# VectorE's order in an attention stage: the combine of the older unit ahead of the row maximum of the newest

## The chip, the cores and the metric

One NeuronCore of a Trainium2 chip runs the whole program. The metric is the device time of one execution in microseconds (us).

## The reference, cut to what matters

The program computes two model blocks in a row on 512 tokens of width 1024 in fp32: an RWKV-7 layer with its feed-forward net, a differential attention layer with its feed-forward net, and then two layers of gated linear attention, spatial gating, retention and pooling. The change concerns the differential attention alone:

```python
s = einsum('bqhd,bkhd->bhqk', q_blk, k) * scale      # 16 half heads of 64
s = where(k_chunk <= q_chunk, s, -inf)               # chunks of 64 tokens
p = softmax(s, axis=-1).reshape(B, 8, 2, Q_BLOCK, S)
p = p[:, :, 0] - lam * p[:, :, 1]                    # the two halves of a head
o = einsum('bhqk,bkhe->bqhe', p, v)                  # v is 128 wide for a head
```

## The kernel before, in words

The kernel is written engine by engine; each engine has its own instruction list, and semaphores order them. The attention stage has 32 units (`N_UNITS`): 8 heads times 4 blocks of 128 queries. Unit i is head i // 4 and query block tq = i % 4 (`unit`, line 914); since the mask is causal in chunks it has tq + 1 key blocks of 128, so 128, 256, 384 or 512 keys. Both halves of the head are worked in one unit.

A unit passes through these steps:

- TensorE, `scores` (line 2836): the scores of both halves, into two PSUM banks (banks 4 and 5 for even units, 2 and 3 for odd ones, `unit_banks`, line 307). It waits until the exponentials of unit i - 2 have read those banks.
- VectorE, `row_max` (line 2142): waits for the scores, writes -1e30 over the masked corner (L2149), reduces both halves to their negative maximum (L2150) and scales it (L2151, `sc_max`).
- ScalarE: waits for `sc_max`, then one exponential for each half (L1586) with its sum as accumulator output; results go to `Pb` (six buffers: three units).
- VectorE, `combine` (line 2155): waits for the exponentials, takes the reciprocal of the second half's sum (L2161), multiplies by -lam and the first half's sum (L2162), and adds the scaled second half to the first (L2165, `pc_ready`). All is kept scaled by the first half's sum, which a later norm takes out.
- TensorE, `transposes` (line 2863): waits for `pc_ready`, transposes the combined block into PSUM bank 6 (L2867).
- ScalarE: copies the transposes to `PTs` (L1598).
- TensorE, `values` (line 2847): multiplies them with the values (L2856). After a head's fourth unit ScalarE copies the output (L1213) and squares it (L1602).

The order on each engine is written out by hand, one iteration p for each unit:

- TensorE (lines 2880 to 2901): half of a piece of the value projection (only p < 24), values(p - 2), the other half, scores(p + 1), transposes(p - 1); from p = 27 on a head sum (L2875) for a later norm.
- VectorE (lines 2168 to 2175): row_max(p), for p = 0 also two key scalings (`key_scale`), then combine(p - 1).
- ScalarE (lines 1570 to 1602): at p = 8, 16 and 24 a copy of projected values and at p = 0, 8 and 16 the rounding of a weight tile (L1202), then the exponentials of p, the output copy, the transposes' copy of p - 1, the squares.
- POOL computes the low part of each weight tile (L1081) once ScalarE has rounded it. SP only loads weights.

Woven into the first 24 units is the rest of the value projection (`value_part`, line 2813): 12 matmuls a unit.

Of the kernel before, what the change touches and what calls it, by code (L numbers as in the profile page):

```python
# [569 lines left out]
def build(nc, t, out):  # L570
# [3 lines left out]
    with ctx:  # L574
# [272 lines left out]
        def wait_job(eng, key):  # L847

            _, who, _, n = JB.info[key]
            eng.wait_ge(job_a if who == "A" else job_d, n)  # L850
# [63 lines left out]
        def unit(i):  # L914

            return i // UNITS_OF_HEAD, i % UNITS_OF_HEAD
# [812 lines left out]
        def _(dve):  # L1729
            seq = [0]  # L1730

            def link(ins):

                seq[0] += 1
                ins.then_inc(dve_seq, 1)
                dve.wait_ge(dve_seq, seq[0])
# [371 lines left out]
            def key_scale(k):  # L2108

                wait_done(dve, ("hinv", k))  # L2110
                dve.tensor_tensor(ak[:, k, :], ak[:, k, :], bank(job_banks(("hinv", k))[0]), ALU.mult
                                  ).then_inc(job_d, 1)
# [29 lines left out]
            def row_max(i):  # L2142

                hd, tq = unit(i)
                b = job_banks(("sc", i))[0]
                N = P * (tq + 1)
                q = 4 + 2 * (i % 3)
                wait_done(dve, ("sc", i))
                link(dve.memset(psum[0:64, b:b + 2, N - CH:N], -1e30))  # L2149
                link(dve.tensor_reduce(col[:, 14:16], psum[:, b:b + 2, 0:N], AX.X, ALU.max, negate=True))  # L2150
                dve.tensor_tensor(col[:, q:q + 2], col[:, 14:16], invq[:, tq, 2 * hd:2 * hd + 2], ALU.mult  # L2151
                                  ).then_inc(sc_max, 1)
                dve.wait_ge(sc_max, i + 1)

            def combine(i):

                hd, tq = unit(i)
                N = P * (tq + 1)
                q = 2 * (i % 3)
                wait_job(dve, ("sc", i))  # L2160
                link(dve.reciprocal(col[:, 17 + q:18 + q], col[:, 17 + q:18 + q]))  # L2161
                link(dve.scalar_tensor_tensor(out=col[:, 17 + q:18 + q], in0=col[:, 17 + q:18 + q],  # L2162
                                              scalar=col[:, 3:4], in1=l1s[:, tq, hd:hd + 1], op0=ALU.mult,
                                              op1=ALU.mult))
                dve.scalar_tensor_tensor(out=Pb[:, q, 0:N], in0=Pb[:, q + 1, 0:N], scalar=col[:, 17 + q:18 + q],  # L2165
                                         in1=Pb[:, q, 0:N], op0=ALU.mult, op1=ALU.add).then_inc(pc_ready, 1)

            for p in range(N_UNITS + 1):
                if p < N_UNITS:
                    row_max(p)  # L2170
                if p == 0:
                    key_scale(6)
                    key_scale(7)
                if p:
                    combine(p - 1)
            sums = l1s[:, :, :].rearrange("p t k -> p (t k)")[:, :, None]
            dve.scalar_tensor_tensor(out=lsq[:, :, :].rearrange("p t (k a) -> p (t k) a", a=2),
                                     in0=sums.to_broadcast([P, TT * HEADS // 2, 2]), scalar=1e-5 * P,
# [958 lines left out]
```

## Time and profile before

| | |
|---|---|
| median of 3 runs | 2244.77 us (2243.22 to 2253.79) |
| profiled execution | 2259.35 us, of it 2257.5 us span |
| busy share: TensorE, VectorE, ScalarE, POOL | 90%, 35%, 36%, 34% |
| attention stage | about 1151 to 1262 us of the span |
| mean granted TensorE clock, share of full | 0.946 |

Times inside a profile count from the start of the span. The busy share of an engine is an average over stages with different limits. PE is TensorE's matmul side, PEld its weight loads, DVE is VectorE, ACT is ScalarE.

### The profile page before, as it was taken

Reading aid. Unit: us, or ns where it says so; the run is one execution under the profiler, and the core shown is the slowest. Engines: PE = TensorE matmul, PEld = TensorE weight load, DVE = VectorE, ACT = ScalarE, POOL = GpSimd, SP = SyncE. Lnnn points to the kernel's source line nnn. Section 1 sums busy time; section 2 is a strip of 40 time slices with the busy share of each in tenths; the row PEclk is TensorE's granted clock in tenths of the full one; section 3 lists DMA queues with packets and bytes.
Section 4 is the critical chain, followed back from the end, with each engine's and each line's share of the span. In section 5 each row is a group of like instructions: output and inputs, shape, how many; then the busy total and the mean of one; then the engine's idle time right before and its main releaser. Section 6 shows DMA issues by size and latency. Waiting matters only on the chain.

```text
span 2257.5 us, 36581 instructions
## 1 busy us (share of the span) xinstructions
PE 2030.8 (90%) x15556; PEld 1559.9 (69%) x15556; DVE 794.1 (35%) x1186; ACT 816.4 (36%) x1056; POOL 774.9 (34%) x644
## 2 busy tenths in 40 slices
PE   5997976668999999989999899999998999969897
PEld 3666766544778888866577578888887876748664
DVE  5576433324322221025666442222002123252233
ACT  6765132232243432132256434343123222242232
POOL 3353322210334444334421134444444432234430
PEclk8998999985999999999999899999999998989999
DMA  4111000020223332312111023333223311122110
GB/s 152 56 50 61 2 4 4 4 61 9 75 75 93 93 101 94 102 58 82 58 55 38 19 75 93 95 92 106 89 84 94 94 46 48 38 79 77 55 56 37
DMA packets 190706, 147.09 MB, mean 65 GB/s; under 512 B 6888, under 2 KB 188351, under 8 KB 190576
## 3 DMA queue, kind: packets, MB, share of 16 engines
q1 hardware_dynamic: 190576, 145.18, 21.0%
q8 instruction: 104, 1.70, 0.3%
q14 instruction: 26, 0.21, 0.0%
HBM read 143.06 MB, written 2.10 MB: 64 GB/s over the span
## 4 chain that ended last, share of the span: by engine, by line
PE 79%; DVE 7%; ACT 5%; issue 4%; POOL 3%; DMA 1%; SPq 0%; ACTq 0%; DVEq 0%
PE psum L2402 21%; PE psum L2404 19%; PE psum L2403 19%; PE psum L2557 4%; POOL w_lo L1081 2%; DVE X_lo L1744 2%; ACT w_hi L1202 1%; PE psum L2478 1%; PE psum L2408 1%; PE psum L2843 1%; PE psum L2782 1%; PE psum L2856 1%; PE psum L2773 1%; PE psum L3044 1%; PE psum L3027 1%
## 5 line engine op out<-in xcount | busy, mean ns | idle before, releaser
L1081 POOL TENSOR_TENSOR w_lo<-weight_raw,w_hi 128x256 fp32r<-128x256 f32 (+5 forms) x588 | 703.4, 1227 | 1254.8 <-ACT w_hi L1202 1254.7
L2402 PE MATMUL psum<-X_hi,w_hi 128*128 128x512 f32 x1528 | 634.5, 415 | 52.6 <-DVE X_lo L1744 33.4
L2404 PE MATMUL psum<-X_hi,w_lo 128*128 128x512 f32 x1528 | 607.5, 398 | 0.0
L2403 PE MATMUL psum<-X_lo,w_hi 128*128 128x512 f32 x1528 | 607.0, 397 | 0.0
L2402 PEld LDWEIGHTS psum<-X_hi,w_hi 128*128 128x128 f32 x1528 | 294.4, 193 | 162.4 <-issue 85.7
L1202 ACT ACTIVATE w_hi<-weight_raw 128x2048 fp32r<-128x2048 f32 (+2 forms) x134 | 249.4, 1862 | 347.4 <-PE psum L2404 336.6
L2403 PEld LDWEIGHTS psum<-X_lo,w_hi 128*128 128x128 f32 x1528 | 294.8, 193 | 66.0 <-issue 8.5
L2404 PEld LDWEIGHTS psum<-X_hi,w_lo 128*128 128x128 f32 x1528 | 293.6, 192 | 64.4
L1793 DVE TENSOR_TENSOR sgate<-rt,psum 128x512 f32<-128x512 f32 x44 | 30.2, 687 | 320.5 <-PE psum L2404 320.5
L2402 PE MATMUL psum<-hb_hi,w_hi 128*128 128x512 f32 x352 | 136.9, 389 | 0.0
L2403 PE MATMUL psum<-hb_lo,w_hi 128*128 128x512 f32 x352 | 136.9, 389 | 0.0
L2404 PE MATMUL psum<-hb_hi,w_lo 128*128 128x512 f32 x352 | 136.9, 389 | 0.0
L2402 PE MATMUL psum<-w_hi,X_hi 128*128 128x256 f32 x384 | 116.3, 303 | 5.6 <-POOL w_lo L1081 3.6
L1187 ACT ACTIVATE sgate<-sgate 128x512 f32<-128x512 f32 x44 | 27.9, 635 | 255.2 <-DVE sgate L1793 255.2
L2403 PE MATMUL psum<-w_lo,X_hi 128*128 128x256 f32 x384 | 110.2, 287 | 0.0
L2404 PE MATMUL psum<-w_hi,X_lo 128*128 128x256 f32 x384 | 110.1, 287 | 0.0
L1783 DVE TENSOR_TENSOR x<-x,psum 128x512 f32<-128x512 f32 x32 | 20.5, 683 | 224.5 <-PE psum L2404 224.5
L2402 PEld LDWEIGHTS psum<-w_hi,X_hi 128*128 128x128 f32 x384 | 75.4, 196 | 12.8 <-issue 12.6
L2403 PEld LDWEIGHTS psum<-w_lo,X_hi 128*128 128x128 f32 x384 | 75.3, 196 | 0.6 <-issue 0.5
L2403 PEld LDWEIGHTS psum<-hb_lo,w_hi 128*128 128x128 f32 x352 | 66.1, 188 | 13.8
L2404 PEld LDWEIGHTS psum<-hb_hi,w_lo 128*128 128x128 f32 x352 | 66.1, 188 | 13.7
L2402 PEld LDWEIGHTS psum<-hb_hi,w_hi 128*128 128x128 f32 x352 | 66.1, 188 | 13.7
(454 smaller groups left out, 2599.7 us busy)
## 6 DMA issues: line engine op xcount, KB each, us to landing
weight_raw<-in_ffn_w_gu SPq DMA_DIRECT2D x88, 512.0 KB, 4.9
weight_raw<-in_l_w_in SPq DMA_DIRECT2D x45, 512.0 KB, 4.7
weight_raw<-in_ffn_w_down SPq DMA_DIRECT2D x40, 512.0 KB, 3.6
weight_raw<-in_kv_w SPq DMA_DIRECT2D x16, 512.0 KB, 4.4
weight_raw<-in_l_w_out SPq DMA_DIRECT2D x16, 512.0 KB, 4.3
weight_raw<-in_rw_w_k SPq DMA_DIRECT2D x8, 512.0 KB, 6.9
weight_raw<-in_rw_w_r SPq DMA_DIRECT2D x8, 512.0 KB, 4.1
weight_raw<-in_rw_w_v SPq DMA_DIRECT2D x8, 512.0 KB, 4.0
```

Of the source, the lines that this page charges most:

```text
L1081: ins = pool.tensor_tensor(l, r, h.bitcast(F32), ALU.subtract)
L1187: act.activation(sgate[:, j, :], sgate[:, j, :], ACT.Silu).then_inc(ff_gate, 1)
L1202: last = act.activation(h, r, ACT.Copy)
L1744: dve.tensor_tensor(X_lo[:, k, :], f, X_hi[:, k, :].bitcast(F32), ALU.subtract).then_inc(xlo_ready, 1)
L1793: dve.tensor_tensor(sgate[:, j, :], rt[:, :], bank(b[0]), ALU.mult).then_inc(ff_raw, 1)
L2402: pe.matmul(ps, wh, xh, start=start, stop=False, skip_group_check=True)
L2403: pe.matmul(ps, wh, xl, start=False, stop=False, skip_group_check=True)
L2404: return pe.matmul(ps, wl, xh, start=False, stop=stop, skip_group_check=True)
L2408: pe.matmul(ps, w, xx[0], start=True, stop=False, skip_group_check=True)
L2478: ins = pe.matmul(bank(6), c_("ones"), square_buffer(i)[:, k % 2, :], start=k == 0, stop=k == KT - 1)
L2557: ins = pe.matmul(out(q, r, k), left(q, r, k), right(q, r, k), start=True, stop=True, skip_group_check=True)
L2773: ins = pe.matmul(psum[0:16, job_banks(key)[0], :], c_("sel64", 16, 16 * i), oT[:, i, :], start=i == first, stop=i == last)
```

## The change

VectorE's loop over the units calls `combine(p - 1)` ahead of `row_max(p)`. The key scalings of p = 0 stay behind row_max(0). The other engines' lists, the semaphores and the buffers are the same.

```diff
             for p in range(N_UNITS + 1):
+                if p:
+                    combine(p - 1)
                 if p < N_UNITS:
                     row_max(p)
                 if p == 0:
                     key_scale(6)
                     key_scale(7)
-                if p:
-                    combine(p - 1)
```

## Rows read from the trace of the kernel before

**Rows 1.** The page's busy time, share of the span and instructions.
```profile
PE 2030.8 (90%) x15556; PEld 1559.9 (69%) x15556; DVE 794.1 (35%) x1186; ACT 816.4 (36%) x1056; POOL 774.9 (34%) x644
```

**Rows 2.** Busy time by stretch: length; engines' busy us (instructions); clock, DMA share, GB/s.
```profile
1215.90:1229.10 13.20, 13.00 (x95) 10.39 (x95) 8.34 (x24) 8.71 (x24) 0.00 (x0) 1.00 0.22 77
1229.10:1240.30 11.20, 9.11 (x58) 6.08 (x58) 8.31 (x24) 8.20 (x23) 0.00 (x0) 1.00 0.00 0
1240.30:1254.00 13.70, 12.44 (x54) 5.94 (x54) 8.37 (x25) 8.39 (x24) 0.00 (x0) 0.88 0.00 1
```

**Rows 3.** Waits, 1157 to 1262 us: us in total, times, longest.
```profile
DVE psum L2149 <- PE psum L2843: 26.4, 21, 2.7
...
PEld psum L2867 <- DVE Pb L2165: 11.7, 17, 1.1
...
PEld psum L2856 <- ACT PTs L1598: 8.1, 13, 0.9
```

**Rows 4.** VectorE's timeline around unit 15: start, us, instruction, idle before it.
```profile
1202.32 0.17 DVE L2149 MEMSET psum<- 64x128 f32 x1 [0.64 <-PE psum L2843]
...
1203.78 0.16 DVE L2151 TENSOR_TENSOR col<-col,invq 128x2 f32<-128x2 f32 x1
...
1205.92 0.16 DVE L2161 RECIPROCAL col<-col 128x1 f32<-128x1 f32 x1
...
1208.61 0.17 DVE L2149 MEMSET psum<- 64x128 f32 x1 [1.49 <-PE psum L2843]
```

**Rows 5.** ScalarE's timeline there: exponentials of unit 15, first of unit 16.
```profile
1203.97 0.78 ACT L1586 ACTIVATE Pb<-psum,col,invq 128x512 f32<-128x512 f32 x1 [0.97 <-DVE col L2151]
...
1205.40 0.20 ACT L1586 ACTIVATION_READ_ACCUMULATOR Pb<-psum,col,invq 128x1 f32 x1
...
1208.58 0.47 ACT L1586 ACTIVATE Pb<-psum,col,invq 128x128 f32<-128x128 f32 x1
```

**Rows 6.** Groups of instructions by shape in the stage: busy us, mean ns, idle before.
```profile
L2150 DVE TENSOR_REDUCE col<-psum 128x2 f32<-128x1024 f32 x6 | 7.3, 1224 | 0.2
...
L2165 DVE SCALAR_TENSOR_TENSOR Pb<-Pb,col 128x512 f32<-128x512 f32 x6 | 4.5, 752 | 0.2
...
L2165 DVE SCALAR_TENSOR_TENSOR Pb<-Pb,col 128x256 f32<-128x256 f32 x7 | 3.4, 484 | 0.2
L2150 DVE TENSOR_REDUCE col<-psum 128x2 f32<-128x256 f32 x6 | 2.5, 425 | 0.2
...
L1586 ACT ACTIVATE Pb<-psum,col,invq 128x512 f32<-128x512 f32 x16 | 12.3, 772 | 7.6 <-DVE col L2151 7.6
...
L1586 ACT ACTIVATE Pb<-psum,col,invq 128x128 f32<-128x128 f32 x16 | 7.2, 466 | 0.0
```

**Rows 7.** VectorE's timeline, row maxima of units 2 and 3.
```profile
1159.07 0.17 DVE L2149 MEMSET psum<- 64x128 f32 x1
...
1162.25 0.17 DVE L2149 MEMSET psum<- 64x128 f32 x1 [0.69 <-PE psum L2843]
```

**Rows 8.** POOL's timeline at unit 16.
```profile
1208.78 5.61 POOL L1081 TENSOR_TENSOR w_lo<-weight_raw,w_hi 128x256 fp32r<-128x256 f32 x8 [21.24 <-ACT w_hi L1202]
```

**Rows 9.** VectorE's timeline: a combine apart from POOL, two instructions beside it.
```profile
1196.94 0.35 DVE L2165 SCALAR_TENSOR_TENSOR Pb<-Pb,col 128x128 f32<-128x128 f32 x1
...
1209.54 0.68 DVE L2151 TENSOR_TENSOR col<-col,invq 128x2 f32<-128x2 f32 x1
...
1210.94 0.79 DVE L2165 SCALAR_TENSOR_TENSOR Pb<-Pb,col 128x128 f32<-128x128 f32 x1
```

**Rows 10.** VectorE's timeline: row maxima of units 23 and 31, the last combine.
```profile
1229.14 0.17 DVE L2149 MEMSET psum<- 64x128 f32 x1 [0.64 <-PE psum L2843]
...
1254.01 0.17 DVE L2149 MEMSET psum<- 64x128 f32 x1 [0.38 <-PE psum L2843]
...
1257.32 0.16 DVE L2161 RECIPROCAL col<-col 128x1 f32<-128x1 f32 x1 [0.59 <-ACT Pb L1586]
```

## The prediction

> **What bounds the kernel now.** I read the page first: TensorE is busy in 90% of the span [rows 1], so a change elsewhere counts only where TensorE comes to wait. The change touches one stage of it: attention over 32 units (a pair of heads times a block of 128 queries), about 1151 to 1262 us, 5% of the run. The second view is the busy time by stretch; I cut at the start of the row maximum of every fourth unit (3, 7, ... 31), since the four query blocks of a head pair have 1, 2, 3 and 4 key blocks and then repeat. In such a round TensorE is busy 13.00 of 13.2 us while the value projection is woven in (units 0 to 23), 9.11 of 11.2 us and 12.44 of 13.7 us in the two rounds after it; VectorE and ScalarE are busy 8.3 to 8.7 us in each [rows 2]. TensorE sets the pace. The third view is the list of waits: VectorE waits 26.4 us for scores, which is slack of VectorE; TensorE's weight loads wait 11.7 us for combined probabilities and 8.1 us for their transposed copies [rows 3]. These last two are what a better order could win.
>
> **The change part by part.** No instruction is added or removed, no DMA moves, and SP's and POOL's queues are untouched. On VectorE the three instructions of combine(p-1) move ahead of the three of row_max(p), for p = 1 to 31; for p = 0 and 32 nothing moves. Gained: transposes(p-1) can start earlier by a row maximum. Added: combine(p-1) waits for exponential p-1 on ScalarE, and now row_max(p) is queued behind that wait. Exponential p waits for row_max(p). So a loop is closed that before was open: row_max(p), exp(p), combine(p), row_max(p+1), each waiting for the one before. Before, row_max(p+1) ran beside exp(p).
>
> Length of the loop for a unit of 512 keys. Row maximum: starts at 1202.32, its last instruction ends at 1203.78 + 0.16, and the exponential starts at 1203.97, so 1.65 with a handoff of 0.03 [rows 4, 5]. Exponentials: 1203.97 to 1205.40 + 0.20 = 1205.60, 1.63, with a handoff 1.66 [rows 5]. Combine: from 1205.92 to 1208.61 less 1.49 of idle = 1207.12, 1.20, with the 0.02 to the next instruction 1.22 [rows 4]. Shorter units: the reduce falls from 1224 to 425 ns, 0.266 for each key block less; an exponential from 772 to 466, 0.102, and there are two; the combine from 752 (512 keys) to 484 (256), 0.134 [rows 6]. Over 4, 3, 2 and 1 key blocks:
> - row maxima 1.65 + 1.38 + 1.12 + 0.85 = 5.00
> - exponentials 1.66 + 1.46 + 1.25 + 1.05 = 5.42
> - combines 1.22 + 1.09 + 0.95 + 0.82 = 4.08
>
> The loop needs 14.50 us for a round. TensorE needs 13.0 or less, so the loop becomes the bound and TensorE waits. Then the sum, from one row maximum start to the next:
> - First round. combine(0) ends at 1159.05 in either order (the next instruction starts at 1159.07; it waited for the first exponential already). From there to the row maximum of unit 3: 1.12 + 1.25 + 0.95 + 1.38 + 1.46 + 1.09 = 7.25, which is 1166.3 against 1162.25 now [rows 7]: **+4.1**.
> - Units 3 to 23, five rounds: now 1229.14 - 1162.25 = 66.89 [rows 7, 10], in the loop 5 x 14.50 = 72.5: **+5.6**.
> - Units 8 and 16: ScalarE copies values and a weight tile between exponentials 7 and 8 (15 and 16). There 1208.58 - 1205.60 = 2.98 pass between the end of one exponential and the start of the next [rows 5], where VectorE's own leg is 1.22 + 0.85 = 2.07. Twice 0.9: **+1.8**. At unit 24 there is no weight tile and the leg of VectorE is the longer one: 0.
> - The same weight tiles start a POOL burst of 5.61 us (8 instructions) [rows 8]. Beside it VectorE's instructions are stretched: 0.68 where the same operation took 0.16, and 0.79 where a combine of the same size took 0.35 [rows 4, 9]. That is 0.52 + 0.44 = 1.0 for each burst. TensorE covers it now; in the loop nothing does. Two bursts (the third is in the first round, in both versions): **+2.0**.
> - Units 23 to 31, two rounds: now 1254.01 - 1229.14 = 24.87 [rows 10], in the loop 29.0: **+4.1**.
> - After row_max(31) both orders are alike: 1254.01 to 1257.32 is 3.31 [rows 10], which is my 1.65 + 1.66: **0**.
>
> The sum is +17.6. For the stretched POOL neighbours there are two ends: 0, if the bursts meet exponentials only, and 0.7 (5.61/8, a whole POOL instruction) for each of the five two-input VectorE instructions that a burst spans, 3.5 for each burst; I keep the 1.0 of the rows, which is the same place in the kernel. The Trainium skill (SBUF — State Buffer, Who interferes with whom) states that a VectorE instruction with two SBUF inputs contends with a GpSimd one that reads SBUF and that the loser is blocked for the whole instruction; by that the sum would be up to 2 x 2.5 = 5.0 higher, while the rows show partial stretches of 0.44 and 0.52.
>
> TensorE's clock is the other unknown. Its granted clock was 1.00 in the woven rounds and 0.88 in the round from 1240.3, which followed a round with waits (9.11 busy of 11.2) [rows 2]; 0.88 is a mix of its two levels, 2.4 and 1.2 GHz. With the loop as bound TensorE waits more in units 24 to 31, so the slow level should show up more. Lower end: 0, as TensorE's slack of several us a round absorbs it. Upper end: at half clock throughout, the work of the two last rounds, 9.11 and 12.44 x 0.88 = 10.9 us, doubles to 40.1 against the 29.0 of the loop, +11. I take about +1.
>
> The sum, near **+18.6**, is against the profiled execution, 2259.35 us (span 2257.5): 2278. That execution is 14.6 above the median of three runs, 2244.77; nothing in my terms lies in that difference, so I carry the same +18.6 to the median: **2263 us**, +0.8%. About 0.5%, 11 us, is what a measurement of this kernel can tell from no change.
>
> **The rivals.**
> - *TensorE is served earlier and the kernel gets faster.* The transposes come earlier by up to 1.65 us, and TensorE's idle time falls. It would win at most the shortfall of TensorE in the rounds: 0.2 in each of five, 2.1 and 1.3 in the last two, about -4, or 2241; with the first round and the end perhaps -7. It decides only if exp(p-1) has ended before the scores of unit p are there, with a combine's length to spare. For it: VectorE does wait 26.4 us for scores, 21 times [rows 3]. Against it: exponential 15 ended at 1205.60, and by then row_max(16) was nearly done: combine(15), which followed it, started at 1205.92 [rows 4, 5]. Behind combine(15) it can't start before 1206.82. And a loop sum of 14.50 can't run in 13.4. Chance 0.03.
> - *The loop is milder than I sum it, and the result is within 0.5%.* If the weight tiles and POOL's bursts fall into ScalarE's part of the loop (both terms zero) and half of the first round's term is covered, 2 + 5.6 + 4.1 = +12 is left; a round of 14.1 instead of 14.5, if some of my durations hold contention that then goes, takes off 3 more: +9, or 2254. For it: the mean durations that I used come from a stage in which all engines are busy. Against it: nothing in the rows shows a shorter one. Chance 0.13.
> - *The clock.* TensorE waits in every unit, drops to 1.2 GHz in the last two rounds and then can't keep up with the loop once the head sums (two matmuls a unit, from unit 27 on) are added: +11 on top, 2274. It decides once TensorE's work in a round, 10.9 us at full clock, passes 14.5, so if over a third of a round is at the low level. For it: the 0.88. Against: the round before it, with its waits, still had 1.00. The Trainium skill (TensorE: Matmul & The Clock Gate, Why this matters for your kernels) warns that idle gaps of TensorE bring the half clock back; it speaks against this change. Chance 0.14.
> - *The forecast*: the loop sets the pace, with its terms as summed, +13 to +24. Chance 0.70.
>
> **How the numbers follow.** Slower by over 0.5%: forecast and clock, 0.84; within: 0.13; faster: 0.03. The range leaves out the faster rival and about half of the mild one at the bottom, and the coincidence of clock and full blocking at the top: +9 to +29, so 2254 to 2274.
>
> **What would show it.** In the changed kernel VectorE's wait for scores (26.4 us) should all but vanish, and a wait of combine's reciprocal for the exponentials should appear, 1.05 to 1.66 a unit, some 40 us in all. ScalarE's wait for the row maximum should be over 30 us; the waits of TensorE's loads for combined probabilities should go to near 0 and those for transposed copies from 8.1 to about 20. The rounds should last 14.5, and 16 to 17 where a weight tile falls in; the stage should end about 18 later. If the rounds stay at 13.4, the step that says exponential and row maximum can't overlap is wrong. If they are 14.5 and the time is still within 0.5%, something behind the stage gave it back. If the last two rounds exceed 30 with a granted clock under 0.8, it was the clock.

## The result, and the profile after

The changed kernel takes 2270.58 us (median of 5 runs, 2264.76 to 2274.22) against 2244.72 us (5 runs, 2243.22 to 2253.79): a ratio of 1.0103, with a 95% interval of 1.0086 to 1.0119, or +19 to +27 us. It is slower, as forecast; the forecast was 2263.

The busy time by stretch of the changed kernel, cut at the row maxima of units 3, 7, 11, 15, 19, 23, 27, 31 and then to 1284 (columns as in [rows 2]):

```profile
1167.30:1182.05 14.75, 13.95 (x103) 11.21 (x102) 8.34 (x24) 8.49 (x24) 0.00 (x0) 1.00 0.01 2
1182.05:1198.46 16.41, 13.59 (x96) 10.50 (x95) 9.38 (x24) 9.96 (x25) 5.60 (x8) 1.00 0.20 65
1198.46:1213.20 14.74, 13.19 (x96) 10.45 (x95) 8.34 (x24) 8.49 (x24) 0.00 (x0) 1.00 0.01 2
1213.20:1229.60 16.40, 14.85 (x96) 11.67 (x95) 9.37 (x25) 10.18 (x25) 5.58 (x8) 0.90 0.20 64
1229.60:1244.34 14.74, 13.19 (x96) 10.45 (x95) 8.33 (x25) 8.49 (x24) 0.00 (x0) 1.00 0.01 2
1244.34:1260.34 16.00, 12.60 (x47) 7.29 (x45) 8.33 (x24) 8.33 (x23) 0.00 (x0) 0.61 0.00 0
1260.34:1275.09 14.75, 14.17 (x59) 6.59 (x58) 8.35 (x25) 8.25 (x23) 0.00 (x0) 0.84 0.00 1
1275.09:1284.00 8.91, 6.71 (x24) 3.42 (x25) 2.81 (x7) 2.60 (x6) 0.00 (x0) 0.81 0.00 0
```

Four rounds, three with the value projection woven in and one without it, have the same length within 0.01 us, 14.74 or 14.75. TensorE's work differs much between them (96 or 103 matmuls against 59), so it isn't TensorE that sets it. The two with a weight tile (and the POOL burst) last 16.4. The round from 1213.20 is one of them, at a granted clock of 0.90, and isn't longer for it. The round from 1244.34 is longer than its equal, at a granted clock of 0.61.

The waits of the changed kernel in the stage (us in total, times, longest), against [rows 3]:

```profile
DVE col L2161 <- ACT Pb L1586: 48.0, 32, 1.8
ACT Pb L1586 <- DVE col L2151: 44.7, 29, 2.7
PEld psum L2856 <- ACT PTs L1598: 22.9, 21, 3.1
...
PEld psum L2867 <- DVE Pb L2165: 1.4, 2, 1.0
...
DVE psum L2149 <- PE psum L2843: 1.3, 1, 1.3
```

VectorE and ScalarE wait for each other, 48.0 and 44.7 us: two engines that take turns. TensorE does get its combined blocks sooner (11.7 before, 1.4 now), which is what the new order gains, but it pays at the next step, the transposed copies (8.1 before, 22.9 now).

VectorE's timeline, a unit of 512 keys and the start of the next in the changed kernel, answers to [rows 4]:

```profile
1198.46 0.17 DVE L2149 MEMSET psum<- 64x128 f32 x1
...
1201.85 0.16 DVE L2161 RECIPROCAL col<-col 128x1 f32<-128x1 f32 x1 [1.76 <-ACT Pb L1586]
...
1203.07 0.17 DVE L2149 MEMSET psum<- 64x128 f32 x1
...
1205.01 0.16 DVE L2161 RECIPROCAL col<-col 128x1 f32<-128x1 f32 x1 [1.12 <-ACT Pb L1586]
```

In the kernel before, combine(14) and row_max(16) stood between row_max(15) and combine(15), and VectorE was not idle from 1202.32 until combine(15) was done. Now row_max(15), 1.76 us of idle, combine(15), row_max(16), 1.12 us of idle, and so on.

ScalarE's timeline at the end of the stage, in the changed kernel and then in the one before, gives the end that I measure the stage by, the last square (L1602):

```profile
1285.24 0.63 ACT L1602 ACTIVATE aq<-oT 128x512 f32<-128x512 f32 x1
```

```profile
1263.17 0.63 ACT L1602 ACTIVATE aq<-oT 128x512 f32<-128x512 f32 x1
```

From the first unit's reduce (1153.73 and 1153.05) to the start of it are **131.5 us, against 110.1**: +21.4. This is the change's effect as a trace shows it, within the interval of the timed runs. The two profiled spans differ by only 11.3 us, because the kernel before lost time behind the stage in its profiled execution. The busy time of the same instructions behind the stage, kernel before, then changed kernel:

```profile
1310.00:2257.00 947.00, 883.10 (x3958) 691.88 (x3956) 251.09 (x377) 294.74 (x323) 350.91 (x301) 0.96 0.24 74
```

```profile
1332.00:2268.00 936.00, 873.83 (x3957) 684.61 (x3955) 250.97 (x377) 294.72 (x323) 350.78 (x300) 0.97 0.24 75
```

About 11 us at a granted clock lower by 0.01, in a part that the change doesn't touch. So this kernel's total moves by that much from one execution to the next, while the length of the stage can be compared to some tenths. The experiments are read by the stage; the ratio stands beside it.

### The profile page after: what moved, and what is told of

It is laid out like the page before. It is cut to its first block, busy times and chain, and to the rows that moved or that the text cites. A ratio compares the mean times of both kernels' runs of the same rounds, so it can differ in the third digit from the quotient of the medians.

```text
span 2268.8 us, 36581 instructions
## 1 busy us (share of the span) xinstructions
PE 2037.0 (90%) x15556; PEld 1563.0 (69%) x15556; DVE 792.8 (35%) x1186; ACT 815.1 (36%) x1056; POOL 775.3 (34%) x644
## 4 chain that ended last, share of the span: by engine, by line
PE 75%; DVE 9%; ACT 8%; issue 5%; POOL 3%; DMA 1%; SPq 0%; DVEq 0%; ACTq 0%
PE psum L2402 20%; PE psum L2404 19%; PE psum L2403 19%; PE psum L2557 4%; POOL w_lo L1081 2%; DVE X_lo L1744 2%; ACT Pb L1586 2%; ACT w_hi L1202 1%; PE psum L2478 1%; DVE col L2150 1%; PE psum L2408 1%; PE psum L2782 1%; PE psum L2773 1%; DVE Pb L2165 1%; PE psum L3044 1%
## 5 line engine op out<-in xcount | busy, mean ns | idle before, releaser
L2404 PEld LDWEIGHTS psum<-w_hi,X_lo 128*128 128x128 f32 x384 | 76.2, 198 | 0.0
L2403 PEld LDWEIGHTS psum<-hb_lo,w_hi 128*128 128x128 f32 x352 | 66.1, 188 | 13.8
```

Of the source, the lines that this page charges most:

```text
L2403: pe.matmul(ps, wh, xl, start=False, stop=False, skip_group_check=True)
L2404: return pe.matmul(ps, wl, xh, start=False, stop=stop, skip_group_check=True)
```

## The experiments

The loop theory: row maximum, exponentials, combine and the next row maximum each wait for the one before, and the length of that loop sets the pace. Its rivals: TensorE at its low clock is the loss; each wait of VectorE for an exponential costs, wherever it is; TensorE, held up by late copies, is the bound. All variants are edits of VectorE's loop unless said otherwise.

| run | stage us | first round, then rounds from unit 3 | ratio (95% interval) |
|---|---|---|---|
| kernel before | 110.1 | 9.4; 13.24 13.58 13.25 13.58 13.24 11.21 13.65 | 1 |
| changed kernel | 131.5 | 13.8; 14.74 16.41 14.74 16.39 14.75 16.00 14.75 | 1.0103 (1.0086 to 1.0119) |
| new_woven_only | 122.9 | 13.8; 14.75 16.42 14.75 16.42 14.75 11.02 12.07 | 1.0086 (1.0048 to 1.0125) |
| new_tail_only | 114.4 | 9.4; 13.23 13.59 13.23 13.59 13.24 14.67 14.75 | 1.0033 (1.0008 to 1.0059) |
| old_two_more | 112.8 | 9.4; 13.75 14.11 13.75 14.10 13.75 12.24 12.75 | 1.0034 (1.0007 to 1.0060) |
| new_two_more | 146.4 | 15.0; 16.81 17.81 16.81 17.82 16.81 17.04 16.99 | 1.0157 (1.0100 to 1.0213) |
| new_from_4 | 126.7 | 9.4; 14.68 16.41 14.75 16.41 14.75 15.27 14.74 | 1.0055 (1.0009 to 1.0101) |
| new_tile_later | 130.4 | 12.0; 14.74 16.04 14.74 16.03 14.74 16.01 14.74 | 1.0119 (1.0073 to 1.0166) |
| old_tile_later | 108.2 | 8.7; 13.59 13.58 13.25 13.59 13.24 11.20 12.08 | 0.9993 (0.9968 to 1.0018) |
| new_odd_only | 120.2 | 12.9; 14.09 14.67 14.08 14.67 14.07 12.67 14.39 | 1.0038 (1.0011 to 1.0066) |
| new_at_3_and_0 | 115.8 | 10.1; 14.01 14.47 14.02 14.46 14.01 13.02 13.03 | 1.0023 (0.9997 to 1.0048) |
| new_where_free | 109.4 | 9.5; 13.74 13.66 13.30 13.66 13.31 11.16 12.15 | 0.9994 (0.9969 to 1.0020) |
| new_copy_first | 144.1 | 13.8; 16.46 18.66 16.47 19.02 16.46 17.50 15.44 | 1.0154 (1.0095 to 1.0214) |

Round lengths are differences of the starts of VectorE's reduces. The granted clock was 1.00 in every round of new_woven_only, new_tail_only, old_two_more, old_tile_later, new_at_3_and_0 and new_where_free. The last round of the kernel before was at 0.87 and that of new_odd_only at 0.88; the last two of the changed kernel, new_two_more, new_tile_later and new_copy_first were at 0.58 to 0.89, and the one from unit 23 in new_from_4 at 0.78.

**One part of the stage at a time.** VectorE's loop in new_woven_only, against the kernel before (in new_tail_only the condition is `p >= 24`):

```diff
+                first = p < 24
+                if p and first:
+                    combine(p - 1)
                 if p < N_UNITS:
                     row_max(p)
...
-                if p:
+                if p and not first:
                     combine(p - 1)
```

> The combine goes first only for p = 1 to 23; from p = 24 on the row maximum goes first again. The closed loop (row maximum, exponentials, combine, each waiting for the one before) is then there in the woven part alone. Loop theory: row maxima of units 7 and 11, 11 and 15 lie 16.4 and 14.7 us apart as in the changed kernel, the last two rounds together take 25 us again in place of 30.8, and the time is 2244.7 + 4.4 + 10.1 = about 2259 to 2261. Clock theory (the loss comes from TensorE at 1.2 GHz in the last units, which the new order's waits bring about): nearly all of it goes, 2245 to 2250.

> The combine goes first only from p = 24 on. Loop theory: rounds of 13.4 us up to unit 23, then two rounds of 30 to 31 us together with a low granted clock, 2244.7 + 6 = about 2251. Clock theory: most of the loss is here, 2260 or more.

Measured: stages of 122.9 and 114.4, +12.8 and +4.3. The rounds of each part are those of the kernel whose order it has. In the timed runs the first is slower by 0.86% and the second by 0.33%; the clock theory, which put nearly all of the loss behind unit 24, falls. The pair also measures what the clock does cost, since neither had a low one in these rounds. Busy time of new_tail_only in the stretch where the changed kernel had 0.61:

```profile
1244.30:1260.30 16.00, 12.83 (x61) 5.79 (x61) 9.54 (x27) 7.55 (x22) 0.00 (x0) 1.00 0.00 1
```

At the full 2.4 GHz the new order needs 14.67 and 14.75 for the two rounds and 8.7 from row_max(31) to the last square; the changed kernel, with stretches at 1.2 GHz, took 16.00, 14.75 and 10.0. So 2.6 us of the changed kernel's stage are clock. The old order, at full clock in new_woven_only, needs 12.07 for the last round, where the kernel before took 13.65: 1.6 us of clock there too, so that the old order at full clock has a stage of 108.5. Against it the two runs cost 14.4 and 5.9, together 20.3, and the changed kernel without its 2.6 us costs 20.4: the two parts add up to the whole.

**The same work added to both orders.** In `row_max`, in either kernel:

```diff
                 link(dve.memset(psum[0:64, b:b + 2, N - CH:N], -1e30))
+                link(dve.memset(psum[0:64, b:b + 2, N - CH:N], -1e30))
+                link(dve.memset(psum[0:64, b:b + 2, N - CH:N], -1e30))
```

> The kernel before (row maximum first), with the masking memset of each unit written three times: 0.40 us more of VectorE work in each of the 32 units, same result. Loop theory: VectorE has 5 us of slack in a round of 13.4, so little of the 12.8 us shows: only where transposes wait for the combine, once a round behind the 512-key row maximum, +2 to +5. If VectorE's own work set the pace already it would be +12 or more.

> The changed kernel with the same two memsets more in each unit, same result. Loop theory: the memset is part of the closed loop, so all of it shows: rounds of 14.74 + 1.6 = 16.3 us, and 2270.6 + 12.6 = about 2283. Clock theory: the extra work falls into VectorE's idle time, +0 to +4.

VectorE's timeline in new_two_more:

```profile
1181.77 0.17 DVE L2149 MEMSET psum<- 64x128 f32 x1
1182.03 0.17 DVE L2150 MEMSET psum<- 64x128 f32 x1
1182.29 0.17 DVE L2151 MEMSET psum<- 64x128 f32 x1
```

A memset more is 0.26, not the 0.20 I had assumed, so 0.52 a unit and 2.08 a round. The new order's rounds without a tile grew from 14.74 to 16.81, by 2.07: all of it. The old order's grew from 13.24 to 13.75, by 0.51: once a round. This is the plainest evidence for the loop: the same VectorE work is exposed four times in a round in one order, and once in the other. It holds in the woven rounds. Those with a tile grew by 1.4 in the new order, since the longer row maximum covers the weight tile: there it ends at 1222.85 and the exponential starts at 1222.97, in the changed kernel 1218.62 and 1219.26. In the last two rounds the old order's 11.2 and 12.1 (at full clock) became 12.24 and 12.75, by 1.0 and 0.7, which is more than once a round. The total of new_two_more also holds more low clock, for its stage ended 11.3 after the last row maximum in place of 10.0.

**The first round alone.** `first = p >= 4`:

> The combine goes first from p = 4 on. Loop theory: first round of 9.4 us as in the kernel before, the rounds from then on 14.7 and 16.4 as in the changed one, and the stage 131.5 - 4.4 = 127 us long. If the first round's 4.4 us only stood for work that comes later anyway, the stage keeps its 131.5.

Measured: 126.7, 4.8 less than the changed kernel, 4.4 in the first round and 0.7 in the round from unit 23 (15.27 against 16.00), less 0.4 after the last row maximum. As expected.

**The weight tile moved.** ScalarE's loop, in either kernel:

```diff
                 if p % PER_STEP == 0 and 1 <= j <= WOVEN:
...
-                if p % PER_STEP == 0 and j < WOVEN:
-                    next_slot(PL.first["kv"] + 1 + j)
...
                     ins.then_inc(job_a, 1)
+                if p % PER_STEP == 0 and j < WOVEN:
+                    next_slot(PL.first["kv"] + 1 + j)
```

> The changed order, and ScalarE rounds the weight tile of p = 0, 8 and 16 behind the exponentials of p instead of ahead of them. The rounds with a tile last 16.4 us in the changed kernel, those without 14.74. If the extra 1.67 is ScalarE's tile in the loop (0.9) plus VectorE instructions stretched beside POOL (the rest), the tile's part goes, as ScalarE then works on it while VectorE combines and takes the next row maximum (1.9 us of it against 0.82 + 1.12): rounds of 15.3 to 15.7, and a stage some 2 to 2.5 us shorter than 131.5. The first round gains too if exponential 0 comes earlier. If POOL is the whole extra, they stay at 16.4.

> The order of the kernel before, with the weight tile behind the exponentials of p. TensorE sets the pace there, with 0.34 us more in rounds with a tile (13.58 against 13.24). If that is the tile ahead of the exponentials, the rounds become 13.24 and the stage 1 us shorter, or 0.7 at the least; the time of the whole does not show it: 0.999 to 1.001 of the kernel before.

Measured in the new order: rounds of 16.04, not 15.3 to 15.7, and a stage 1.1 shorter, not 2 to 2.5. The first round gained 1.8 and the two with a tile 0.7, but the stretch after the last row maximum, at a granted clock of 0.68 in place of 0.81, lost 1.5. The tile is out of the way, but POOL's burst starts later with it and meets longer VectorE instructions. VectorE's timeline there in new_tile_later, then the instructions beside the burst in the changed kernel:

```profile
1193.92 0.92 DVE L2165 SCALAR_TENSOR_TENSOR Pb<-Pb,col 128x256 f32<-128x256 f32 x1
...
1196.24 0.59 DVE L2151 TENSOR_TENSOR col<-col,invq 128x2 f32<-128x2 f32 x1
```

```profile
1220.57 0.32 DVE L2162 SCALAR_TENSOR_TENSOR col<-col,l1s 128x1 f32<-128x1 f32 x1
1220.92 0.79 DVE L2165 SCALAR_TENSOR_TENSOR Pb<-Pb,col 128x128 f32<-128x128 f32 x1
...
1222.66 0.35 DVE L2151 TENSOR_TENSOR col<-col,invq 128x2 f32<-128x2 f32 x1
...
1224.54 0.53 DVE L2162 SCALAR_TENSOR_TENSOR col<-col,l1s 128x1 f32<-128x1 f32 x1
```

0.92 where the mean was 0.484 [rows 6], and 0.59 where 0.16 is usual: 0.87 of the 1.3 us that a round with a tile still costs more. The rest is smaller pieces: a stretch of 0.10 at 1193.56, the exponentials of unit 17 held 0.13 by the copy that now stands behind the tile, and row_max(18) waiting 0.21 for scores. In the changed kernel the four stretched instructions hold 0.10 + 0.44 + 0.19 + 0.31 = 1.04 (usual: 0.22, 0.35, 0.16, 0.22), and the tile on ScalarE the other 0.6 of the 1.66: row_max(16) ends at 1218.62, and the exponential behind the tile starts at 1219.26, 0.64 later where 0.04 is usual.

In the old order the rounds with a tile kept 13.58, so that expectation failed too. The traces show why: moving the tile behind the exponentials of p leaves it ahead of the copy of the transposes of p - 1, and it is that copy for which TensorE waits. TensorE's timeline at values(15) in the kernel before, and at values(7) in old_tile_later:

```profile
1210.12 1.16 PE L2856 MATMUL psum<-PTs,av 128*128 128x128 f32 x8 [0.32 <-ACT PTs L1598]
```

```profile
1184.42 1.16 PE L2856 MATMUL psum<-PTs,av 128*128 128x128 f32 x8 [0.32 <-ACT PTs L1598]
```

The wait is 0.32 of the 0.34 in both. The tile is the cause, and the place tried was no better. The stage's 1.9 us less is mostly the last round at full clock (12.08 against 13.65). The total is not changed.

**Some places only.**

`first = p % 2 == 1`:

> The combine goes first for odd p only. Loop theory: the loop is closed over one unit and open over the next: row maximum of p + 1 (even) runs beside exponential p. A round in which every second link is cut needs less than TensorE's 13.0, so it comes back to 13.2 to 13.8 us, stage 110 to 116. If any wait of VectorE on the exponentials is what costs, whatever follows it, half the loss stays: rounds near 14.2, stage about 121.

`first = p % 4 == 3 or p % 4 == 0`:

> The combine goes first only for p = 3, 7, ... and 4, 8, ...: behind the exponentials of the 384 and 512 key units, which end last. Loop theory: these places carry the loss, rounds of 14.2 us or more and 15.3 or more with a weight tile, stage 119 to 127. If each place costs the same, 16 of 31 give 11 us, stage 121, and new_where_free would show its share too.

`first = p % 4 == 2 or p % 8 == 5`:

> The combine goes first only where, in the trace of before, the older unit's exponential ends a combine's length ahead of the scores of the newest: p = 2, 6, 10, ... and p = 5, 13, 21, 29. Loop theory: a link in the loop costs only where VectorE would otherwise have worked on the row maximum at once; here it waited anyway, so rounds of 13.2 to 13.7 us and a stage of 109 to 111.5 us, no gain either, as TensorE is full. If any combine put first costs (the odd-p run lost half of the whole for half of the places), 12 of 31 places give 4 to 8 us.

Against the 108.5 of the old order at full clock, new_where_free costs 0.9 us for 12 places, new_at_3_and_0 7.3 for 15 (the expectation counts p = 32 too, where nothing moves), new_odd_only 11.7 for 16, and the changed kernel, without its 2.6, 20.4 for 31. Part of the 11.7 is clock: the last round of new_odd_only was at 0.88, and a last round at 0.87 cost the old order 1.6, so my estimate for it at full clock is 10 to 12.

new_where_free met the loop's expectation, and not the 4 to 8 us of a cost at every place: a combine put first is nearly free where VectorE would have waited for scores anyway. The other two missed the loop's numbers. new_at_3_and_0 is lower (115.8, expected 119 to 127; rounds of 14.0 and 14.5, expected 14.2 or more and 15.3 or more), new_odd_only higher (120.2, expected 110 to 116, and near the 121 of its rival). A cost for each place doesn't fit the whole either: new_where_free and new_at_3_and_0 together hold 27 of the 31 places, and their sum, 8.2, is far from 20.4.

The loop of two engines is cut in both runs, so another ring must set the 14.0 and 14.1. The trace of new_odd_only shows it in the round from unit 11. VectorE, ScalarE, then VectorE again:

```profile
1198.63 0.17 DVE L2149 MEMSET psum<- 64x128 f32 x1
```

```profile
1201.81 0.49 ACT L1598 ACTIVATE PTs<-psum 128x384 f32<-128x384 f32 x1
```

```profile
1208.79 0.17 DVE L2149 MEMSET psum<- 64x128 f32 x1 [2.95 <-PE psum L2846]
...
1212.71 0.17 DVE L2149 MEMSET psum<- 64x128 f32 x1
```

row_max(11) starts late, behind combine(10) (1198.63), and with it the exponentials of unit 11, which end at 1201.92. Only then does ScalarE copy the transposes of unit 10, for which TensorE waits 0.42 us. From 1202.35 to 1208.61 TensorE is busy without a break (6.26 of 6.26 us), and the scores of unit 14 come at the end of that stretch. row_max(14), the exponentials of unit 14 and combine(14) follow one another, and row_max(15) stands behind combine(14) at 1212.71, though its scores were there at 1211.58. That closes the ring: 3.29 + 0.43 + 6.26 + 0.18 + 2.80 + 1.12 = 14.08. In new_at_3_and_0 the round from unit 11 has the same members, and TensorE's stretch is again 6.26 of 6.26 us (1198.27 to 1204.53). So in both runs one place of each round, p = 3, 7, ..., stands in the ring that sets the pace, and new_where_free has none of these places. This is read from one woven round of each run; why the rounds from unit 23 and the first round differ between the two (12.67 and 14.39 against 13.02 and 13.03, 12.9 against 10.1) stays open.

**The copies ahead of the exponentials.** On ScalarE, with the counts of its semaphore changed to match:

```diff
+                if 0 <= p - 1 < N_UNITS:
+                    key = ("pt", p - 1)
+                    wait_done(act, key)
+                    n = P * (unit(p - 1)[1] + 1)
+                    act.activation(PTs[:, (p - 1) % 2, 0:n], bank(job_banks(key)[0], n), ACT.Copy).then_inc(job_a, 1)
                 if p < N_UNITS:
...
-                if 0 <= p - 1 < N_UNITS:
-                    key = ("pt", p - 1)
...
```

> The changed order on VectorE, and ScalarE copies the transposes of p - 1 ahead of the exponentials of p. TensorE's waits for those copies (22.9 us on its loads, 16.1 us on its matmuls in the changed kernel) should fall by over half, as the copy no longer stands behind the exponential. Loop theory: they are a consequence and not the bound, so rounds without a tile keep 14.7 us (14.6 to 15.0). If the copies behind late exponentials are what holds TensorE up and through it everything, the rounds fall to 13.6 or less and the stage to under 120.

Waits of new_copy_first:

```profile
ACT PTs L1584 <- PE psum L2867: 58.0, 29, 3.6
...
PEld psum L2856 <- ACT PTs L1584: 6.1, 10, 1.1
```

Measured: TensorE's waits for copies fell as expected, from 22.9 to 6.1, but the rounds rose to 16.46. Neither theory said that. ScalarE now waits 58.0 us for transposes, ahead of the exponential: the loop got TensorE's transposes as one more member. That TensorE's waits for copies all but went and nothing was gained speaks against the late copies as the bound, but the edit put another wait in their place, so this run alone doesn't show it. The rounds of one length in the changed kernel, with 96 or 103 matmuls and with 59, are the better evidence.

## Why the prediction was right

The sign, the mechanism and the range were right; the size was 18.6 where the trace has 21.4 and the runs 19 to 27.

| step | predicted | measured | from |
|---|---|---|---|
| first round | +4.1 | +4.4 | 13.8 against 9.4 |
| units 3 to 23 | 5.6 + 1.8 + 2.0 = +9.4 | +10.1 | 77.0 against 66.9 |
| units 23 to 31 | +4.1, clock +1 | +5.9 | 30.75 against 24.87 |
| after row_max(31) | 0 | +1.0 | 10.0 against 9.0 |
| stage | +18.6 | +21.4 | |

- **The loop.** I summed 14.50 for a round; it is 14.74. This is the first of two mis-sized terms, 0.24 in each of seven rounds, 1.7 us. ScalarE's and VectorE's rows of the changed kernel show where it is:

```profile
1214.86 0.78 ACT L1586 ACTIVATE Pb<-psum,col,invq 128x512 f32<-128x512 f32 x1 [2.57 <-DVE col L2151]
...
1216.29 0.20 ACT L1586 ACTIVATION_READ_ACCUMULATOR Pb<-psum,col,invq 128x1 f32 x1
```

```profile
1216.59 0.16 DVE L2161 RECIPROCAL col<-col 128x1 f32<-128x1 f32 x1 [1.76 <-ACT Pb L1586]
```

  The exponentials take the 1.63 that I had (1214.86 to 1216.49), but the reciprocal starts 0.10 after their end. I had used 0.03, which is the handoff in the other direction, and also what the one late reciprocal of [rows 10] shows (1257.29 to 1257.32). Four times 0.07 is 0.28 a round.
- **Weight tile and POOL.** 1.9 a round predicted (0.9 and 1.0), 1.66 found: 0.6 and 1.04. The stretches were partial, as the rows of before had them. ScalarE also copies projected values ahead of the exponentials at p = 4, 12 and 20, which the description of the kernel leaves out; the rounds that hold such a copy are no longer (14.75, 14.74, 14.75) than the last, which holds none (14.75). The Trainium skill (SBUF — State Buffer, Who interferes with whom) has the loser blocked for the whole GpSimd instruction; by that each of these four would have been up to 0.7 longer, 2.8 in all, and the traces show 0.10 to 0.44. A VectorE instruction that comes while a POOL instruction is part way through would wait less than the whole 0.7, so these numbers don't contradict the page.
- **The clock.** This is the second mis-sized term. +1 was taken for the new order, on top of its 29.0; measured like that it is 2.6 (1.3 in the round from unit 23, 1.3 after row_max(31)). That the two kernels differ by 2.6 - 1.6 = +1.0 in clock is luck, as the 24.87 that I compared with already held the old order's 1.6. The rival gave the clock up to +11: it fell to 0.61 and 0.84 in the last two rounds, but TensorE's slack took nearly all of it. Only once did VectorE wait for scores:

```profile
1256.35 0.17 DVE L2149 MEMSET psum<- 64x128 f32 x1 [1.28 <-PE psum L2843]
```

- **Last two rounds.** At full clock on both sides they cost 29.5 - 23.3 = +6.2 and not +4.1: 1.6 is the clock in the old order's last round, and the longer loop is the rest. After row_max(31) the new order at full clock is not equal but 0.3 shorter (8.7 against 9.0).
- **The whole.** The 2.8 us between 18.6 and 21.4 are 1.7 for the loop, 1.6 for the clock and 0.3 in the first round, less 0.5 for tile and POOL and 0.3 at the end. The errors partly cancelled.
- **The signs of the loop** all came: the wait for scores 26.4 to 1.3, the reciprocal's wait 48.0 (about 40 forecast), ScalarE's 44.7 (over 30), the copies' 22.9 (about 20). But so did the sign that I had set for the clock: the last two rounds took 30.75, over 30, at granted clocks of 0.61 and 0.84. It was set too near the loop's own 29.5 to tell the two apart; new_tail_only does, with 29.4 at 1.00. The mild rival ("within 0.5%") had durations that would shrink without contention; none of the means of [rows 6] fell by more than 0.01.

No version tried beats both kernels. new_where_free and old_tile_later have stages within 1 us of the old order at full clock, and totals at 0.9994 and 0.9993 with 1 inside each interval.

## What to carry to other kernels

When two steps on one engine are swapped, ask what each waits for, and whether a step that used to run beside another engine's work now stands behind it. If the waits then form a ring, add up the ring and compare it with what the bounding engine needs for the same work: here 14.7 against 13.2. Cutting such a ring in some places can leave a longer one that runs through the third engine, as in new_odd_only. A step that is ready earlier for the engine that bounds is worth nothing if the next piece of work for it comes later; and a loop's length can be checked cheaply by adding a known small instruction to it in both orders.

## What the runs showed of the hardware that was not expected

- VectorE's reciprocal started 0.10 us after the accumulator read it waited for (1216.49 to 1216.59), ScalarE's exponential 0.04 after VectorE's product (1214.82 to 1214.86). In the kernel before one such start took 0.03 (1257.29 to 1257.32) [rows 10], another 0.10. Over all 13 traces the instruction ahead of it tells them apart: every reciprocal that came directly behind a row maximum and waited for ScalarE took 0.10 (208 of them), every one behind a combine or a key scaling 0.03 (38). In the code `row_max` ends with one more wait on a semaphore than `combine`; that this wait costs the 0.07 wasn't tried.
- Beside the POOL burst in the changed kernel VectorE's instructions with two inputs in SBUF were stretched (0.32 for 0.22, 0.79 for 0.35, 0.35 for 0.16, 0.53 for 0.22), while the reciprocals (0.16) and the reduces from PSUM (0.69 at 1221.93) kept their time.
- An added memset of 0.17 us costs 0.26 from start to start where another memset follows it, 0.20 where the reduce does.
- The total of the kernel before moved from 2235.94 to 2268.43 over the comparisons, with the same program; in the one pair looked at, 11 us lay in a stretch whose granted clock differed by 0.01.
